# Key-key product of the mixer written to the bank of the new values instead of a bank of the scores

## The reference

```python
m = where(strict, einsum("bnhid,bnhjd->bnhij", k_beta, k) * decay, 0)    # key-key
sol = triangular_solve(m, concat([v_beta, k_beta * exp(gc)]), unit_diagonal=True)
attn_intra = einsum("bnhid,bnhjd->bnhij", q, k) * decay                  # key-query
...
v_new = u_i - w_i @ state
o = q_i @ state + a_i @ v_new
state = state * cd_i + k_i^T @ v_new
```

## Time and profile before

| | |
|---|---|
| time, median of 3 runs | 1521.15 us (1514.58 to 1523.36) |
| the profiled execution | 1524.07 us, of which its span is 1522.3 us |
| PE busy | 1448.2 us, 95% |
| DVE, ACT, POOL busy | 749.4, 560.4, 672.4 us |
| mean granted clock of PE | 0.973 |

### The profile page before, as it was taken

How to read it: one execution, slowest core, us unless ns; L and a number is a source line. 1 busy time by engine, 2 the same in 40 slices (tenths; PEclk the granted TensorE clock), 3 DMA queues, 4 the chain that set the end, 5 groups by cost and what they waited for, 6 DMA issues and landing times.

```text
span 1522.3 us, 24218 instructions
## 1 busy us (share of the span) xinstructions
PE 1448.2 (95%) x9201; PEld 1210.2 (79%) x9201; DVE 749.4 (49%) x1280; ACT 560.4 (37%) x1309; POOL 672.4 (44%) x623
## 2 busy tenths in 40 slices
PE   5999999999996999899999879999999999999997
PEld 4878888888885888788888768888888888888886
DVE  5004535554553577775223955434444354354436
ACT  5223444444343344443334432232332322422334
POOL 4112323232333545754333573463453543634656
PEclk9999999999997798998999999999999999999999
DMA  5112223332323232221533011211202202112103
GB/s 180 44 54 65 73 80 85 107 102 60 85 67 120 70 103 64 72 88 50 194 91 103 28 28 56 56 52 35 81 28 56 79 33 56 56 56 56 50 35 124
DMA packets 144643, 111.19 MB, mean 73 GB/s; under 512 B 5568, under 2 KB 132112, under 8 KB 144528
## 3 DMA queue, kind: packets, MB, share of 16 engines
q1 hardware_dynamic: 144384, 109.11, 23.8%
q10 hardware_dynamic: 144, 0.52, 0.1%
HBM read 88.63 MB, written 20.99 MB: 72 GB/s over the span
## 4 chain that ended last, share of the span: by engine, by line
PE 88%; DVE 7%; issue 2%; DMA 1%; ACT 0%; POOL 0%; SPq 0%; DVEq 0%; POOLq 0%
PE banks L289 10%; PE banks L291 9%; PE banks L290 9%; PE banks L1924 8%; PE banks L1925 8%; PE banks L1926 8%; PE banks L1945 5%; PE banks L1944 5%; PE banks L1943 5%; PE banks L679 2%; PE banks L988 1%; PE banks L656 1%; PE banks L1042 1%; PE banks L1007 1%; DVE area L2106 1%
## 5 line engine op out<-in xcount | busy, mean ns | idle before, releaser
L289 PE MATMUL banks<-act_h,w_h 128*128 128x512 f32 x624 | 251.5, 403 | 0.0
L281 POOL TENSOR_TENSOR w_l<-w_raw,w_h 128x1024 fp32r<-128x1024 f32 x49 | 121.3, 2476 | 290.1 <-ACT w_h L277 290.1
L291 PE MATMUL banks<-act_h,w_l 128*128 128x512 f32 x624 | 245.0, 393 | 0.0
L290 PE MATMUL banks<-act_l,w_h 128*128 128x512 f32 x624 | 244.6, 392 | 0.0
L2050 POOL TENSOR_TENSOR w_l<-area,w_h 128x512 fp32r<-128x512 f32 x102 | 141.9, 1396 | 160.7 <-ACT w_h L1963 160.7
L2050 POOL TENSOR_TENSOR w_l<-w_raw,w_h 128x512 fp32r<-128x512 f32 x86 | 117.7, 1373 | 167.3 <-ACT w_h L1963 167.3
L2200 DVE TENSOR_TENSOR area<-area,banks 128x512 f32<-128x512 f32 x176 | 120.8, 687 | 121.9 <-PE banks L1945 120.0
L289 PEld LDWEIGHTS banks<-act_h,w_h 128*128 128x128 f32 x624 | 118.2, 189 | 27.1 <-issue 3.5
L291 PEld LDWEIGHTS banks<-act_h,w_l 128*128 128x128 f32 x624 | 118.0, 189 | 25.8
L290 PEld LDWEIGHTS banks<-act_l,w_h 128*128 128x128 f32 x624 | 118.2, 189 | 22.7
L1924 PE MATMUL banks<-act_h,w_h 128*128 128x512 f32 x320 | 125.3, 391 | 7.8 <-POOL w_l L2050 7.8
(11 more groups left out here) (259 smaller groups left out, 2792.3 us busy)
## 6 DMA issues: line engine op xcount, KB each, us to landing
w_raw<-in_w_in SPq DMA_DIRECT2D x31, 512.0 KB, 4.0
area<-in_x SPq DMA_DIRECT2D x8, 1024.0 KB, 9.8
projected_tm<-area SPq DMA_DIRECT2D x32, 256.0 KB, 2.9
w_raw<-in_w_out SPq DMA_DIRECT2D x16, 512.0 KB, 4.1
w_raw<-in_w_gate SPq DMA_DIRECT2D x12, 512.0 KB, 4.1
area<-in_w_down SPq DMA_DIRECT2D x12, 512.0 KB, 3.9
w_raw<-in_w_up SPq DMA_DIRECT2D x12, 512.0 KB, 4.6
projected_cm<-area SPq DMA_DIRECT2D x20, 256.0 KB, 2.2
```

The costliest lines, as they stand in the source:

```text
L281: e.tensor_tensor(w_l[:, b], w_raw[:, b], w_h[:, b].bitcast(F32), ALU.subtract).then_inc(sems["wl_ready"], 1)
L289: e.matmul(dst, w_h[:, b, k], act_h[:, k, cols], start=(k == 0), stop=False)
L290: e.matmul(dst, w_h[:, b, k], act_l[:, k, cols], start=False, stop=False)
L291: mm = e.matmul(dst, w_l[:, b, k], act_h[:, k, cols], start=False, stop=(k == KT - 1))
```

## The change

`key_key(c)` writes bank 4, which the key-state product and the new values share, and no longer bank 2. Its wait for all score copies of chunk c - 2 (`h_sc`) gives way to a wait for the ACT copy of the new values of chunk c - 2 (`vn`). `with_decay` reads bank 4. `key_state(c)` now waits for `m` (that `with_decay` of chunk c + 1 has read bank 4) in place of `vn`, and `scores(c, 0)` no longer waits for `m`. No instruction that computes is added, removed or moved in any engine's order.

```diff
@@ key_state(c)
                 reach(e, "s_new", c)
-                reach(e, "vn", c)
+                reach(e, "m", min(c + 2, NT))
@@ scores(c, q)
                 if q == 0:
-                    reach(e, "m", min(c + 2, NT))
                     reach(e, "at0", min(c + 2, NT))
@@ key_key(c)
                 e.wait_ge(sems[f"kt_loaded{c % 2}"], 16 * (c // 2 + 1))
-                reach(e, "h_sc", NQ * (c - 1))
+                reach(e, "vn", c - 1)
                 for h in range(DNH):
-                    mm = e.matmul(bank(2)[:, h * P:(h + 1) * P], kT[:, c % 2, h, :], kT[:, c % 2, h, :], start=True, stop=True)
+                    mm = e.matmul(bank(4)[:, h * P:(h + 1) * P], kT[:, c % 2, h, :], kT[:, c % 2, h, :], start=True, stop=True)
@@ with_decay(c)
-                    ins = e.scalar_tensor_tensor(out=mm_[:, h, :], in0=bank(2)[:, h * P:(h + 1) * P], scalar=d_all[:, c, h:h + 1],
+                    ins = e.scalar_tensor_tensor(out=mm_[:, h, :], in0=bank(4)[:, h * P:(h + 1) * P], scalar=d_all[:, c, h:h + 1],
```

## The result

The changed kernel took 1527.44 us (median of 16 runs, 1512.37 to 1533.96) against 1516.32 us of the kernel before (16 runs, 1512.37 to 1531.62). The ratio is 1.0051, 95% interval 1.003 to 1.0071: slower by half a percent, about 8 us (the means are 8.2 us apart, the medians 11.1), where I forecast 2.8 us less. The median lies above my range of 1511.7 to 1523.4. Over the whole study four executions far above the others of their kernel, 1540.7 to 4515.6 us, three of the kernel before and one of e16, are left out of ratios and means.

The account below looks back on a forecast made before the run. PE was taken to bound the kernel (88% of the chain that ended last). Gains of 1.62 us in steps 1, 3 and 5 and 1.20 in step 2 sum to 2.82, taking 1521.15 to 1518.3 us, range 1511.7 to 1523.4.

Parts of the forecast that it names:

- The local steps: Mixer steps 1, 3 and 5 at full clock: early key_key gains 0.75 us, loses 0.21, net 0.54 each.
- won up to m_turn: End of a full-clock mixer step: key_key fills PE's stall, so m_turn starts 0.75 us earlier.
- causal stretches update(v, 0): DVE, end of step: update(v, 0) runs beside POOL's causal and stretches to about 0.5 us.
- lost between m_turn and the level-1 update: End of step: update(v, 0) ends at 564.73 instead of 564.52 beside causal, a loss of 0.21 us.
- forecast step of 28.1 us: Mixer: full-clock steps last about 28.1 us in place of 28.6.
- Key_state met no new wait: Mixer, PE queue: key_state's new wait for `m` costs nothing, because m_turn just ahead waits for the same count.
- C: Mixer, first queries: DVE caught behind POOL in steps 0, 1, 3 and 5 costs 6.1 us, 1524.4; chance 0.05.
- D: Mixer: nothing arrives; the stall moves whole to update(u, 6) or DVE gives time back, 1521.2 us; chance 0.13.
- fed without stalls after the mixer: After the mixer: PE has no stalls up to the end, so what is won in the mixer arrives.
- the term at zero: Mixer clock: slow stretches carried over unchanged from the profile before, adding nothing to the forecast sum.
- rival B: Mixer clock: one more step turns slow, 1522.9 us, two make 1527.4; chance 0.10; slower result 0.05.
- rival A: Mixer clock: less idling keeps step 2 at full clock, gain 6.7 us, 1514.4; chance 0.27.

Follow-up runs that it names:

- e16: Kernel before with one product of the new values made twice; ratio 0.9994 to the kernel before.
- e4: Changed kernel with half of the first scores piece and the level-5 update made twice, filling two PE idle times; ratio 0.9968 to the kernel before.
- e1: Kernel before, unchanged, run again; ratio 1.0008 to the kernel before.
- e2: Changed kernel, unchanged, run again for a second profile; ratio 1.0046 to the kernel before.
- e17: Changed kernel, unchanged, run again on one chip with its one-product-twice variant; ratio 1.0054 to the kernel before.
- e3: Changed kernel with key_key in the new bank but the old wait for score copies put back; ratio 1.0001 to the kernel before.
- either fill alone: Changed kernel with only half of the first scores piece made twice, 1.0006, or only the level-5 update made twice, 0.9993, to the kernel before.
- the first fill: Changed kernel with half of the first scores piece made twice, ahead of the level-1 update; alone, ratio 1.0006 to the kernel before.
- e10: Kernel before with DVE's final_sb moved ahead of pack(v, 0); ratio 0.9981 to the kernel before.
- e18: Changed kernel with one product of the new values made twice; ratio 1.0000 to the kernel before.
- e9: Changed kernel with DVE's final_sb moved ahead of pack(v, 0); ratio 0.9977 to the kernel before.

## Why the prediction was wrong

**The local steps held.** Key_key starts with no wait, 0.83 us are won up to m_turn at full clock (forecast 0.75; the signalling from pack to the next product was 0.10 and not 0.14, and the rest is rounding of modelled ends), causal stretches update(v, 0) to 0.56 us (forecast 0.50), and 4.72 - 4.46 = 0.26 of it is lost between m_turn and the level-1 update (forecast 0.21). Net 0.57, forecast 0.54. The Trainium skill's rule that I cited, an exclusive lock between DVE and POOL (page "SBUF — State Buffer"), agrees with the 0.56 us. The forecast step of 28.1 us at full clock is that of e4. Key_state met no new wait, nor did key_key. Rivals C and D did not happen: the first queries of a step took 1.62 and 1.60 us at full clock in steps 0 and 5, and the time between the last copy and m_turn did shrink. One sentence of the prediction was wrong without weight: PE is not fed without stalls after the mixer, it waits 7.8 us once for POOL (L1924, near 890 us) in the trace of before. The wait is 7.8 and 7.7 us in e1 and e4, whose steps 7 begin 3 us apart, so it moves with the mixer's end and swallows nothing there.

**What failed was the term at zero.** I carried the clock over unchanged: the sum held every slow stretch of the trace before at its place, and of rival B I wrote that "the shorter stalls speak against it". They were hardly shorter in sum in the first pair (15.1 against 15.5 us), one of them had grown (0.56 to 0.84 us) and had falls behind it, and where they were shorter, in e2 (11.8 against 14.0 in e1), the clock was the lower one; a slow PE also waits less, so that sum follows the clock as much as it leads it. B happened, and not once or twice but up to once a step: 27.8 us became 30.5. A step loses 2.7 us by it, about five times the 0.57 that the change wins there. I had seen that "moving things can as well spoil a good step", and still gave B twice or more no more than 0.05. That the measured 1527.44 is the 1527.4 worked out for B twice is chance: the sum started from 1521.15, the median of three runs, and sixteen gave 1516.32, 4.8 us less.

**That the loss is the clock's is shown.** Over 353 executions of the study, taken together with an offset of its own for each kernel, the time falls 1.00 us (0.04 of standard error) for each 0.001 of mean granted clock, with a scatter of 2.4 us. The 16 runs of the changed kernel have a mean clock of 0.9667, the kernel before 0.9727 over its runs in all jobs. By that slope it is 6.0 us of loss; what is left at equal clock is a gain of 0.7 us, give or take 1.4, and jobs differ by up to 3 us at equal clock, so this is no measure of the gain. Within e2's job it is 0.0072 of clock, 7.2 us by the slope, and 7.8 measured between the means; within e17's 0.0091, 9.1 by the slope, and 8.3 measured.

**That the early start of key_key causes it is shown** (e3 against e2), and so is that it takes no removal of one certain wait to undo it: either fill alone takes it away within the noise, both together turn it round, and 0.27 us more work a step takes 8 us off. That some of the falls come from the grown wait of 0.84 us is made likely by the count (11 of 21 such waits, none of 81 shorter ones), not by an experiment that changes this wait alone: the first fill covers part of it and adds work. What I argue and have not shown is why e2 and e17 fall in every step: a slow stretch lengthens its step there by two to three microseconds, and in e2 and e17 the next step then meets the fall at the same place again, so that one pattern keeps itself alive, while in the kernel before a slow and a fast step take turns. What stays open is a rule that gives the clock from the length and the waits of a step: e10 and e4 have full-clock steps of one length (28.05 and 28.06 us), and clocks of 0.0015 below and 0.0050 above that of before.

**The rule on the clock.** The page "TensorE: Matmul & The Clock Gate", section "A second HAM failure mode: psum-queue depth-cycling", of the Trainium skill ties a clock that swings to short idles of PE. I took it as a reason for a gain, rival A, because I took the idle time to shrink. The rows agree with it in part: both fills raised the clock from 0.9673 to 0.9795 in one job. They do not where e18 raised it by 0.0080 against e17 with work added where PE does not wait, nor where e2 has less idle time than e1 and the lower clock. So the rule gave no sign for this change, and my reading of it was a guess.

## What to carry to other kernels

Before you count a removed wait as a gain in a kernel whose PE clock falls now and then, give the clock a term of its own, with a price and a chance either way; here it cost more than twice the gain that was forecast. List PE's waits after the change as well as before, and look at those that have grown. Neither their sum nor the length of a full step told how the clock would come out. A single profile cannot decide this: time both kernels in many executions and read each one's mean clock. Filling PE's waits with harmless repeats and moving DVE's work off the chain took this kernel to 0.9943, where the removed wait is worth 0.2% by my sum, and one pair of runs (e9 and e10) shows as much, barely clear of noise.

## What was not expected of the hardware

The granted clock of PE answers to changes far below a microsecond. One 128 x 128 product more in a step of 28 us, 0.27 us, raised the mean clock from 0.9649 to 0.9729 on one chip; three more in the kernel before, over six executions, went with 0.9675 where that kernel had 0.9708. In the profiled executions of e2 and e17 the falls came once a step and steps 1 to 5 lasted 30.4 to 30.8 us; in the kernel before (e1) they came every second step, near 528, 586 and 644 us. And at one place in the step the clock fell behind 11 of 21 waits of 0.84 us and behind none of 81 waits of 0.12 to 0.61 us.
